# A two-layer block and its second stage on one core: the last four output tiles move from the triangular inverse into the group norm's waits

## The reference, cut to what matters

```python
    y = ((y - mean) * lax.rsqrt(var + GN_EPS)).reshape(B, S, RWKV_WIDTH) * ln_g + ln_b
    y = y + bonus.reshape(B, S, RWKV_WIDTH)
    y_a = y * jax.nn.silu(g)
...
        y = jnp.concatenate([y_a, y_b, y_c], axis=-1)
        x = x + y @ w_out[i]
        gate = jax.nn.sigmoid(rms_norm(x, ple_norm_g[i]) @ ple_w_gate[i])
        x = x + gate * (p[i] @ ple_w_proj[i])
```

## Time and profile before

| | us |
|---|---|
| median of 3 executions | 2543.86 |
| lowest and highest | 2543.39, 2543.96 |
| span of the profiled execution, first to last instruction | 2542.3 |
| PE busy in it | 2256.6 (89%) |
| DVE, ACT busy in it | 960.2, 463.7 |

### The profile page before, as it was taken

How to read it: one execution, slowest core, us unless ns; L and a number is a source line. 1 busy time by engine, 2 the same in 40 slices (tenths; PEclk the granted TensorE clock), 3 DMA queues, 4 the chain that set the end, 5 groups by cost and what they waited for, 6 DMA issues and landing times. The chain is left out here.

```text
span 2542.3 us, 43732 instructions
## 1 busy us (share of the span) xinstructions
PE 2256.6 (89%) x18641; PEld 1175.6 (46%) x18641; DVE 960.2 (38%) x1752; ACT 463.7 (18%) x911; POOL 230.2 (9%) x181
## 2 busy tenths in 40 slices
PE   6989988879998898887898977899879979999998
PEld 3543436634463343763444433577634444444442
DVE  1057784332026767533224551444322241111112
ACT  1021431120102142111122341422110200000000
POOL 0021300000020320000004530500000000000000
PEclk9999989989999999998989987999989989999999
DMA  4134011020315300102201101120113549999997
GB/s 152 65 143 166 9 46 36 19 84 33 107 48 199 116 18 29 36 19 83 76 17 67 34 25 54 50 63 20 39 51 124 234 195 403 421 422 422 422 422 297
DMA packets 65228, 334.82 MB, mean 132 GB/s; under 512 B 7712, under 2 KB 11296, under 8 KB 36256
## 3 DMA queue, kind: packets, MB, share of 16 engines
q1 hardware_dynamic: 65056, 332.32, 34.2%
HBM read 322.06 MB, written 5.77 MB: 129 GB/s over the span
## 5 line engine op out<-in xcount | busy, mean ns | idle before, releaser
L422 PE MATMUL ps<-store,side_ring 128*128 128x512 f32 x784 | 397.9, 630 | 25.6 <-DMA side_ring<-in_w_out 9.4
L2417 PE MATMUL ps<-expert_ring,xe 128*64 128x512 f32 x1024 | 224.8, 597 | 2.7 <-DVE back L2526 1.7
L422 PEld LDWEIGHTS ps<-store,side_ring 128*128 128x128 f32 x784 | 137.2, 195 | 181.2 <-issue 148.5
L335 PE MATMUL ps<-store,side_ring 128*128 128x512 f32 x384 | 170.2, 606 | 1.9 <-DVE store L301 1.9
L2417 PEld LDWEIGHTS ps<-expert_ring,xe 128*64 128x64 f32 x1024 | 73.3, 138 | 150.8 <-issue 148.7
L422 PE MATMUL ps<-store 128*128 128x512 f32 x224 | 115.4, 648 | 23.3 <-DMA store<-in_w_merge 22.7
L335 PEld LDWEIGHTS ps<-store,side_ring 128*128 128x128 f32 x384 | 74.7, 195 | 96.3 <-issue 94.2
L2445 PE MATMUL ps<-expert_ring,store 128*64 128x512 f32 x512 | 113.2, 601 | 1.4 <-DVE store L2502 1.4
L1502 PE MATMUL ps<-store,weight_ring 128*128 128x512 f32 x256 | 110.7, 593 | 1.9 <-DVE store L301 1.9
L2474 ACT ACTIVATE store<-ps 128x1024 f32<-128x1024 f32 x16 | 16.4, 1025 | 419.4 <-PE ps L2417 419.4
L511 POOL TENSOR_TENSOR attn_z<-attn_z,tables 128x512 f32<-128x512 f32 (+1 forms) x24 | 37.6, 1569 | 568.5 <-PE ps L500 566.3
(11 more groups left out here) (424 smaller groups left out, 3840.5 us busy)
## 6 DMA issues: line engine op xcount, KB each, us to landing
expert_ring<-in_w_expert SPq DMA_DIRECT2D x192, 1024.0 KB, 16.3
mixed<-in_w_ada SPq DMA_DIRECT2D x24, 1024.0 KB, 4.8
side_ring<-in_w_attn SPq DMA_DIRECT2D x32, 512.0 KB, 3.7
side_ring<-in_w_rwkv SPq DMA_DIRECT2D x20, 512.0 KB, 4.4
weight_ring<-in_ple_gate SPq DMA_DIRECT2D x16, 512.0 KB, 4.4
store<-in_w_merge SPq DMA_DIRECT2D x14, 512.0 KB, 3.9
side_ring<-in_w_conv SPq DMA_DIRECT2D x12, 512.0 KB, 3.4
chosen<-in_w_o SPq DMA_DIRECT2D x8, 512.0 KB, 5.6
```

What stands on the lines that cost most here:

```text
L335: last = nc.tensor.matmul(ps[:, u, :], ring[:, u, k, :], src[:, k, :], start=(k == 0), stop=(k == kt - 1))
L422: ins = self.nc.tensor.matmul(self.ps[:, self.banks[j % banks], :], self.ring[:, j % self.slots, k, :], self.src[:, k, :], start=(k == 0), ...
L2417: last = nc.tensor.matmul(ps[w, 2 * ep + half, :], xe[:, ep, k, :], ring[:, unit % SLOTS, k2, S * half:S * half + S], start=(k == 0), stop ...
```

## The change

Tiles 4 to 7 are no longer made and added to `x` beside `invert`; its side work is an empty list. In their place, SP loads their weights for blocks 3 to 7 during the blocks phase, into parts of `h` and of `M.tables` that are free by then. The group norm becomes a function, `group_norm`, inside the `together` block. In its waits PE starts tiles 4 to 7 (`begin`: five products each, with no stop) in banks 7, 4, 5 and 6, and leaves them open. A new `finish_projection` takes the place of `add_projection`: it adds the products with blocks 0 to 2 to the four open tiles, then makes tiles 0 to 3, all in eight banks, and waits per block of `y`. `norm` takes `x` in that order. The order of the embedding tiles, their banks, and the grain of the last DVE passes change too.

```diff
-def norm(..., meanwhile=None, bank=7):
+def norm(..., meanwhile=None, bank=7, order=range(KT)):
...
-            with phase(nc, made=0, taken=0, gated=0) as (block, s):
+            with phase(nc, made=0, taken=0, gated=0, late_landed=0) as (block, s):
+                @block.sync
+                def _(sp):
+                    for j in range(EARLY_OUT, KT):
+                        sp.dma_start(late(j), w_out(j)[:, RP:KT, :]).then_inc(s["late_landed"], 16)
+                    sp.wait_ge(s["late_landed"], 16 * (KT - EARLY_OUT))
...
-            out_ring = sbt("side_ring", [P, 3, KT - RP, P])
-            side = SideProjection(nc, M, [add(j) for j in range(EARLY_OUT, KT)], KT - RP, y[:, RP:KT, :], out_ring, 3, (0, 1))
+            side = SideProjection(nc, M, [], KT - RP, y[:, RP:KT, :], None, 1, (0, 1))
             invert(nc, M, pairs_of(low), pairs_of(inv), pairs_of(inv_t), NCH // 2, 2 * RP, 1, side, "vector")
...
+def group_norm(nc, M, y, bonus, gate, late, proj, emb, embedded, col):
...
+            def begin(j):
+                for k in range(RP, KT):
+                    nc.tensor.matmul(ps[:, out_bank(j), :], late(j)[:, k - RP, :], y[:, k, :], start=(k == RP), stop=False)
...
+            for j in range(RP):
+                nc.tensor.matmul(ps[:, j, :], M.c("head_ones"), y[:, j, :], start=True, stop=True).then_inc(s["mean_made"], 1)
+            begin(EARLY_OUT)
+            for j in range(RP):
+                pe.wait_ge(s["squared"], j + 1)
+                nc.tensor.matmul(ps[32 * j:32 * j + 32, 3, :], M.c("head_rows"), sq[:, j, :], start=True, stop=True).then_inc(s["var_made"], 1)
+            begin(EARLY_OUT + 1)
+            begin(EARLY_OUT + 2)
+            pe.wait_ge(s["root"], 1)
+            for j in range(RP):
...
+            embed(0)
+            begin(EARLY_OUT + 3)
+            for j in range(1, BEFORE):
+                pe.wait_ge(s["scaled"], j)
+                embed(j)
...
+BEGUN_FIRST = tuple(range(EARLY_OUT, KT)) + tuple(range(EARLY_OUT))
+def finish_projection(nc, M, weights, src, x, ready, embed_kept):
...
+            for n, j in enumerate(BEGUN_FIRST):
+                pe.wait_ge(s["landed"][n % 4], 16 * (n // 4) + 16)
+                if n == KT - EARLY_OUT:
+                    pe.wait_ge(embed_kept, BEFORE)
+                for k in range(RP):
+                    if n == 0:
+                        pe.wait_ge(ready, k + 1)
+                    last = nc.tensor.matmul(ps[:, out_bank(j), :], ring[:, n % 4, k, :], src[:, k, :],
+                                            start=(j < EARLY_OUT and k == 0), stop=(k == RP - 1))
+                last.then_inc(s["tile_done"], 1)
...
                 with together(nc):
+                    ready, kept = group_norm(nc, M, y, bonus, mixed_z[:, R_G:R_G + RP, :], late, proj, emb, embedded, col)
                     embed = embedding(nc, M, a["ple_proj"][layer], a["p"][layer])
-                    added = add_projection(nc, M, lambda j: w_out(j)[:, 0:RP, :], KT, RP, y[:, 0:RP, :], x)
-                    ready = norm(nc, M, x, lambda k: col("ple_g", k), h, source=added,
+                    added = finish_projection(nc, M, lambda j: w_out(j)[:, 0:RP, :], y, x, ready, kept)
+                    ready = norm(nc, M, x, lambda k: col("ple_g", k), h, source=added, order=BEGUN_FIRST,
```

More of the change, by code:

```diff
@@ L250, in load, with norm @@
     return s["loaded"], 16 * len(pairs)
-def norm(nc, M, src, gain, out, scratch=None, shift=None, source=None, params=None, meanwhile=None, bank=7):
+def norm(nc, M, src, gain, out, scratch=None, shift=None, source=None, params=None, meanwhile=None, bank=7, order=range(KT)):
     total, wide = M.ps[:, bank, 0:P], M.ps[:, bank, :]
@@ L263, in _ @@
             def _(act):
-                for k in range(KT):
+                for n, k in enumerate(order):
                     if source:
-                        act.wait_ge(source[0], source[1] + k + 1)
+                        act.wait_ge(source[0], source[1] + n + 1)
                     nc.scalar.activation(squares[:, k, :], src[:, k, :], ACT.Square).then_inc(s["squared"], 1)
@@ L277, in _ @@
             def _(pe):
-                for k in range(KT):
-                    pe.wait_ge(s["squared"], k + 1)
+                for n, k in enumerate(order):
+                    pe.wait_ge(s["squared"], n + 1)
                     for q in range(4):
                         last = nc.tensor.matmul(total[32 * q:32 * q + 32], M.c("ones")[:, 0:32], squares[:, k, q * P:(q + 1) * P],
-                                                start=(k == 0), stop=(k == KT - 1), tile_position=(0, 32 * q))
+                                                start=(n == 0), stop=(n == KT - 1), tile_position=(0, 32 * q))
                 last.then_inc(s["summed"], 1)
@@ L1202, with out_bank, rwkv_branch @@
 EARLY_OUT = 4
-def rwkv_branch(nc, M, x, h, y, raw, z, dg, maxima, sums, up, w_gate, w_out, w_proj, p_layer, embedded, col):
+def out_bank(j):
+    return j if j < EARLY_OUT else 7 if j == EARLY_OUT else j - 1
+def rwkv_branch(nc, M, x, h, y, raw, z, dg, maxima, sums, up, w_gate, w_out, w_proj, p_layer, bonus, proj, emb, late, col):
     ps = M.ps
@@ L1209, in rwkv_branch @@
         sb = lambda name, shape: buffer(nc, outer, name, shape)
-        at, bt, kt_, bonus = (sb(x, [P, RP, S]) for x in ("rw_a", "rw_b", "rw_k", "bonus"))
+        at, bt, kt_ = (sb(x, [P, RP, S]) for x in ("rw_a", "rw_b", "rw_k"))
         end_decay = sb("end_decay", [P, RP, NCH])
         r, k, v = z[:, R_R:R_R + 3, :], z[:, R_K:R_K + 3, :], z[:, R_V:R_V + 3, :]
-        proj = h[:, 0:BEFORE // 2, :].rearrange("p u n -> p (u n)").rearrange("p (j k c) -> p j k c", j=BEFORE, k=2)
-        emb = h[:, 2:4, :]
         add = lambda j: (w_out(j)[:, RP:KT, :], lambda dve, made: nc.vector.tensor_tensor(x[:, j, :], made, x[:, j, :], ALU.add))
@@ L1349, in _ @@
                                                 ALU.mult).then_inc(s["state_ready"], 1)
[L1352 to L1413, removed]
@@ new lines, with _ @@
+BEGUN_FIRST = tuple(range(EARLY_OUT, KT)) + tuple(range(EARLY_OUT))
+def finish_projection(nc, M, weights, src, x, ready, embed_kept):
+    ps = M.ps
+    ring = buffer(nc, None, "weight_ring", [P, 4, RP, P])
+    with phase(nc, landed=4, tile_done=0, added=0) as (block, s):
+        @block.sync
+        def _(sp):
+            for n, j in enumerate(BEGUN_FIRST):
+                if n >= 4:
+                    sp.wait_ge(s["tile_done"], n - 3)
+                sp.dma_start(ring[:, n % 4], weights(j)).then_inc(s["landed"][n % 4], 16)
+        @block.tensor
+        def _(pe):
+            for n, j in enumerate(BEGUN_FIRST):
+                pe.wait_ge(s["landed"][n % 4], 16 * (n // 4) + 16)
[7 more added lines that the diff above has]
+                last.then_inc(s["tile_done"], 1)
+        @block.vector
+        def _(dve):
+            for n, j in enumerate(BEGUN_FIRST):
+                dve.wait_ge(s["tile_done"], n + 1)
+                nc.vector.tensor_tensor(x[:, j, :], ps[:, out_bank(j), :], x[:, j, :], ALU.add).then_inc(s["added"], 1)
+    return s["added"], 0
```

58 lines of the change are left out of this document (57 added, 1 removed).

## The result

The changed kernel takes 2504.57 us (median of 4 executions, 2499.95 to 2507.85) against 2543.62 beside it: a ratio of 0.985, 95% interval 0.9838 to 0.9863. So it is 39 us faster, where 54.9 + 0.2 = 55 were forecast: 16 us over the forecast of 2489, and 1.6 over the range's upper end, 2503. The profiled execution took 2499.95 us.

A forecast was written before the change was run, and what follows sets the result against it. The prediction took side products on PE's path to bound the inverse, and waits the group norm and projection stage. From 2543.86 us it took 54.9 for the inverses and 0.2 for the stage, giving 2489, range 2479 to 2503.

The forecast's parts named there:

- Its steps: Inverse without side products: two steps take 2.87 us through PE and DVE, so 1.435 each, just above PE's own 1.40.
- The longer chain: Rival: the inverse's steps have a longer chain than seen, 2.0 us, giving 15.8 back, so 2505 us; chance 0.07.
- The side products lay in PE's waits: Rival: removing side products from the inverse gains only its start, 4.54 + 2.08 us per layer, so 2530; chance 0.03.
- The inverse's start: Inverse, layer 1: DVE's four copies end at 421.70, set by the inverse's own transfers; PE's 4.54 us weight wait goes.
- the weights' new place: Blocks phase: four transfers open it and cost nothing; without that cover they would cost 4.54 us a layer.
- Its end: Inverse's last steps: steps 18 and 19 stay at 1.40 us, 20 and 21 take 0.70 without a side product.
- The group norm with the projection: Last stage: PE works without waits, 50.4 us instead of 51.57 and 51.50; net of semaphore clears, 0.2 us gained.
- TensorE at 1.2 GHz: Rival: the clock falls once 128x512 products leave the inverse, slowing it and perhaps the recurrence, so 2584 us; chance 0.03.
- the old wait that comes back elsewhere: Rival: begun products delay the group norm's chain past PE; a whole old wait per layer gives 2520 us; chance 0.03.

The follow-up runs named there:

- The probe: Changed kernel with a TensorE-only phase in front, 24 inverse steps with a 128x512 product each, then 24 without: 2.60 us a step, then 1.99.
- the repeat: The changed kernel run once more, unchanged, beside the kernel before on another occasion: 2503.33 us, ratio 0.9856.

## Why the prediction was wrong

- **"Its steps"** is the step that failed. It took two limits, PE's own 1.40 us and the chain of 2.87 us for two steps, and gave 1.435. Neither is what failed: 1.40 shows at about every second step, and DVE can follow at 1.29. A third limit was not in the list, the supply of instructions, and it gave 2.04 and 2.21. In the sum, 14 x (2.04 - 1.435) = 8.5 and 14 x 0.775 = 10.9 us went missing. The inverse takes (from its first product, in layer 2 from DVE's first copy, to its last DVE instruction) 43.20 us in place of 61.90 and 44.66 in place of 61.23: 18.7 and 16.6 us less of the 27.3 and 27.6, 19.6 short in the sum, nearly all of it from the steps.
- The evidence for 1.40 was one step without a product among steps that had one. It ran on instructions fetched ahead during the 2.60 us steps around it. The probe shows the same at its change: for 5 us behind 78.3 PE still runs without a pause, the first one ends at 83.21.
- A page of the Trainium skill, Runtime: NRT & Kernel Launch, section Instruction fetch mechanics, says that instructions come in blocks of 256, that crossing a block's boundary is mostly hidden, and that the fetch hides behind a floor of about 20 cycles for each instruction. The blocks of 256 agree with the trace. The rest does not: PE used 144 instructions in 1.40 us, 9.7 ns each, the supply gave one per 3.7 / 256 us = 14.5 ns, and the probe's second half lost 30% to it (1.99 against 1.40). The measurement decides.
- **The longer chain** as a rival named 2505 us, and that time came by luck. Its mechanism did not: a longer chain leaves the mean spacing at 2.05 to 2.14, and the pauses lie inside a step.
- **"The side products lay in PE's waits"** was too high with its 2530 us, but holds in part. Before the change PE had no such wait; with the products gone, waits for instructions take their place. By the table the move takes 11.7 us a layer out of the inverse, not 20 x 1.20 = 24.0.
- **The inverse's start** held: the copies end at 421.35 (forecast 421.70), and PE had no wait for weights, so "the weights' new place" held too. Its end took somewhat longer: the last four spacings are 5.1 us together (451.07 to 456.21), where 2 x 1.40 + 2 x 0.70 = 4.2 were forecast.
- **The group norm with the projection** held step by step: spread at 16.8 us behind the first mean product (16.5), 3.9 behind the root (3.3), `y` 4.2 before the projection (4), first add at 31.9 (31.4), the whole 0.2 above its 50.4, clock 1.00. Of the begun products fifteen stand ahead of the spread (five of them ahead of the variances), as the prediction's sum has it, and not ten.
- **TensorE at 1.2 GHz** and the old wait that comes back elsewhere both fell: 1.00 in the whole inverse, no gap in the last stage.
- The range had no term for such a limit; its steps went up to 1.61 only. Its own sum, 2488.8 + 14.9, ends at 2503.7, not 2503.
- The sum with the measured inverses is 2543.6 - 35.3 - 0.9 - 0.9 = 2506.5, 2 us over the median. The profiled span fell by 44.1, 7 more than that; most of these lie in stretches that the change leaves alone, and they come and go between executions (the repeat's span is 2502.1).

## What to carry to other kernels

A rate read from one short step between long ones is not the rate of a row of such steps: what was fetched, filled or buffered meanwhile pays for it. Before filler is taken out of a stream of small products, count the stream's instructions and set them against the pulses of the instruction queue: here 144 per step at 3.7 us per 256 make 2.1 us, so by this estimate 0.57 of a 128x512 product per step (0.68 / 1.20) finds room. 10 products on 22 steps left the spacing as it was, 15 did not. That is why 10 of 20 products in the inverse and 10 in the group norm's waits (2492 us) beat both all moved (2503) and none moved (2511).

## What the runs showed of the hardware

Small products can starve TensorE of instructions at the full clock with no semaphore in sight. The signs are "issue" pauses of 0.2 to 1.4 us on PE, up to 1.5 on its weight loads, in the midst of a run of equal products, and a 16 KB block on the instruction queue every 3.4 to 4.1 us without let-up, where in the probe's first half 3.8 to 5.1 us go between blocks that are not waited for. The surest sign is the count: 256 instructions from pause to pause, in the settled part of the inverse 252 to 256.

In the probe's settled pauses the records of single transfers show one block at a time. A block's transfer takes 0.9 to 1.5 us, PE goes on 2.3 to 2.9 us after its start, and the transfer of the next block starts 1.0 to 1.2 us after that. Why this takes so long is open: whether the fetch waits for PE to use up a block, or for something else, was not tried.
